# A hybrid attention and delta-rule layer: the fourth merged chunk transposed by DMA instead of by TensorE

## The reference, cut to what matters

```python
D_MODEL = 2048; SEQ = 256                      # x: (1, 256, 2048) float32
h = rms_norm(x, norm_gain)
aq, ak, av, az, bqkv, bz, bbeta, balpha, gate_a, gate_b = jnp.split(h @ w_in, cuts, axis=-1)
ya = moba_attention(heads(aq), heads(ak), heads(av)) * jax.nn.silu(az)          # 256 x 1024
yb = ...   # gated delta rule of bqkv, per-head RMSNorm, * silu(bz)              # 256 x 1024
merged = (jax.nn.sigmoid(gate_a) * (ya @ w_branch_a)
          + jax.nn.sigmoid(gate_b) * (yb @ w_branch_b))                          # 256 x 2048
x = x + merged @ w_out                                                           # 256 x 2048
return rms_norm(x, final_norm_gain)
```

## Time and profile before

| | |
|---|---|
| median of three runs | 771.9 us |
| the profiled execution | 772.16 us |
| its span in the profile | 770.4 us |
| TensorE busy | 758.4 us, 98% |
| VectorE / ScalarE / GpSimd busy | 73% / 60% / 16% |
| DMA queue of SyncE and ScalarE | 153.53 MB, 74% of the 16 engines' time |
| mean granted TensorE clock | 0.997 |

### The profile page before, as it was taken

One profiled execution on the slowest core, in us unless ns is written; L12 is line 12 of the kernel. 1 busy time (PEld: TensorE's weight loads), 2 busy tenths in 40 slices (PEclk: granted clock), 3 DMA queues, 4 the chain that ended last, 5 costly groups with the idle time before them and its releaser, 6 DMA issues.

```text
span 770.4 us, 10402 instructions
## 1 busy us (share of the span) xinstructions
PE 758.4 (98%) x3483; PEld 625.7 (81%) x3483; DVE 564.8 (73%) x1265; ACT 464.9 (60%) x697; POOL 122.1 (16%) x179
## 2 busy tenths in 40 slices
PE   8999999999999999999999999999999999999995
PEld 6888888888888888888888888888888888887884
DVE  5769847975895689479758956894798476966563
ACT  5686647656765675476657657764856663535441
POOL 6112011110101021101111120201021002512120
PEclk9999999999999999999999999999999999999998
DMA  9968767886788786778866786778676586798643
GB/s 254 241 170 219 205 163 214 193 217 179 184 209 198 192 208 181 199 192 197 212 174 203 200 217 170 203 188 215 174 213 182 181 222 182 217 331 268 190 153 109
DMA packets 225572, 154.44 MB, mean 200 GB/s; under 512 B 55408, under 2 KB 190576, under 8 KB 225392
## 3 DMA queue, kind: packets, MB, share of 16 engines
q1 hardware_dynamic: 225376, 153.53, 74.0%
q10 hardware_dynamic: 144, 0.26, 0.1%
HBM read 140.64 MB, written 2.11 MB: 185 GB/s over the span
## 4 chain that ended last, share of the span: by engine, by line
PE 95%; DMA 2%; issue 1%; DVE 1%; SPq 1%; ACT 0%; POOLq 0%; POOL 0%; DVEq 0%; ACTq 0%
PE pj L633 29%; PE pj L631 29%; PE pj L632 29%; DMA w_raw<-in_w_out_dram 1%; PE dn_ps L676 1%; PE pj L871 1%; PE pj L870 1%; PE pj L869 1%; DMA w_raw<-in_w_in_dram 1%; PE dn_ps L690 0%; PE dn_ps L685 0%; PE mo_ps L717 0%; PE dn_ps L677 0%; DVE w_lo L1169 0%; PE mo_ps L721 0%
## 5 line engine op out<-in xcount | busy, mean ns | idle before, releaser
L1169 DVE TENSOR_TENSOR w_lo<-w_raw,w_hi 128x1024 fp32r<-128x1024 f32 x251 | 312.6, 1250 | 138.1 <-ACT w_hi L885 137.1
L631 PE MATMUL pj<-w_hi,xt_hi 128*128 128x512 f32 x860 | 345.9, 402 | 1.2 <-DVE w_lo L1169 1.2
L633 PE MATMUL pj<-w_hi,xt_lo 128*128 128x512 f32 x860 | 336.6, 391 | 0.0
L632 PE MATMUL pj<-w_lo,xt_hi 128*128 128x512 f32 x860 | 335.8, 390 | 0.0
L885 ACT ACTIVATE w_hi<-w_raw 128x1024 fp32r<-128x1024 f32 x251 | 263.2, 1055 | 114.4 <-PE pj L633 88.3
L633 PEld LDWEIGHTS pj<-w_hi,xt_lo 128*128 128x128 f32 x860 | 161.4, 188 | 34.3
L631 PEld LDWEIGHTS pj<-w_hi,xt_hi 128*128 128x128 f32 x860 | 161.7, 188 | 33.5 <-issue 0.9
L632 PEld LDWEIGHTS pj<-w_lo,xt_hi 128*128 128x128 f32 x860 | 161.8, 188 | 31.4
L1356 DVE SCALAR_TENSOR_TENSOR xs<-lrep,xs 128x31 f32<-128x31 f32 (+30 forms) x496 | 88.9, 252 | 0.0
L550 POOL TENSOR_TENSOR xo<-v,own 128x128 f32<-128x128 f32 x16 | 13.6, 847 | 139.4 <-DVE v L1365 99.1
L1296 DVE SCALAR_TENSOR_TENSOR conv<-kk,hs,conv 128x255 f32<-128x255 f32 (+2 forms) x72 | 29.7, 480 | 0.0
(11 more groups left out here) (292 smaller groups left out, 760.6 us busy)
## 6 DMA issues: line engine op xcount, KB each, us to landing
w_raw<-in_w_in_dram SPq DMA_DIRECT2D x384, 256.0 KB, 3.3
w_raw<-in_w_out_dram SPq DMA_DIRECT2D x64, 256.0 KB, 4.0
w_raw<-in_w_branch_a_dram SPq DMA_DIRECT2D x32, 256.0 KB, 3.8
w_raw<-in_w_branch_b_dram SPq DMA_DIRECT2D x32, 256.0 KB, 3.7
gate<-in_x_dram SPq DMA_DIRECT2D x8, 256.0 KB, 5.2
gate<-in_x_dram SPq DMA_DIRECT2D x4, 512.0 KB, 7.7
gate<-in_final_norm_gain_dram SPq DMA_DIRECT2D x1, 1024.0 KB, 10.3
out_dram<-gate SPq DMA_DIRECT2D x4, 256.0 KB, 3.5
```

The costliest lines, as they stand in the source:

```text
L631: pe.matmul(bank[:, t, :], hi[:, k, tok], w_hi[:, slot, cs], start=(k == 0), stop=False)
L632: pe.matmul(bank[:, t, :], hi[:, k, tok], w_lo[:, slot, cs], start=False, stop=False)
L633: mm = pe.matmul(bank[:, t, :], lo[:, k, tok], w_hi[:, slot, cs], start=False, stop=(k == kt_all - 1))
L1169: dve.tensor_tensor(w_lo[:, slot, :], w_raw[:, slot, :], w_hi[:, slot, :].bitcast(F32), ALU.subtract).then_inc(lo_ready, 1)
```

## The change

Chunk 3 goes the way of chunks 0 to 2. M_TURNED gets a fourth entry, 231, so that the SyncE queue waits for the last m_apart behind the load of unit 231 and issues the DMA transpose there, ahead of the reload of x, the final gain and unit 232. GpSimd's loop runs over all four chunks. turn_merged_last, its semaphore and its PSUM operands are gone, and the final gain waits for m_apart, which the queue has waited for already.

```diff
-M_TURNED = [FIRST_B + BU * (c + 1) + 7 for c in range(NC - 1)]
+M_TURNED = [FIRST_B + BU * (c + 1) + 7 for c in range(NC)]
...
                     for j in range(NC):
                         sp.dma_start(gate[:, j, :, :], x[:, j * CH:(j + 1) * CH].rearrange("(t p) n -> p t n", p=P)
                                      ).then_inc(x_again, 16)
 
-                    sp.wait_ge(mT_done, 2)
+                    sp.wait_ge(m_apart, T * NC)
                     sp.dma_start(gate[:, NC:NC + NC // 2, :, :].rearrange("p c t n -> p (c t n)"),
...
             pool.wait_ge(vb_ready, T * H)
-            for c in range(NC - 1):
+            for c in range(NC):
                 for t in range(T):
                     pool.wait_ge(merged, T * c + t + 1)
...
-            def turn_merged_last():
-                pe.wait_ge(merged, T * NC)
-                for half in range(2):
-                    for q in range(4):
-                        i, t = 2 * half + q // 2, q % 2
-                        mm = pe.transpose(mo_ps[:, (4 * half + q) * P:(4 * half + q + 1) * P],
-                                          gate[:, 2 * NC - 1, t, i * P:(i + 1) * P], ident[:, :])
-                    mm.then_inc(mT_done, 1)
...
-                    if c == 0 and j == 2:
-                        turn_merged_last()
...
             def merged_hi(c):
                 for half in range(2):
-                    if c < NC - 1:
-                        act.wait_ge(m_joined, 2 * c + half + 1)
-                    else:
-                        act.wait_ge(mT_done, half + 1)
-                    m = (mT if c < NC - 1 else mo_ps)[:, half * CH:(half + 1) * CH]
+                    act.wait_ge(m_joined, 2 * c + half + 1)
+                    m = mT[:, half * CH:(half + 1) * CH]
...
             def merged_lo(c):
-                m = mT if c < NC - 1 else mo_ps
                 for half in range(2):
                     dve.wait_ge(mT_hi_ready, 2 * c + half + 1)
                     ks = slice(4 * c + 2 * half, 4 * c + 2 * half + 2)
-                    dve.tensor_tensor(xt_lo[:, ks, :].rearrange("p k t -> p (k t)"), m[:, half * CH:(half + 1) * CH],
+                    dve.tensor_tensor(xt_lo[:, ks, :].rearrange("p k t -> p (k t)"), mT[:, half * CH:(half + 1) * CH],
```

More of the change, by code:

```diff
@@ L260, in build @@
         m_apart, m_joined = sem("m_apart"), sem("m_joined")
-        mT_done, mT_hi_ready, mT_lo_ready = sem("mT_done"), sem("mT_hi_ready"), sem("mT_lo_ready")
+        mT_hi_ready, mT_lo_ready = sem("mT_hi_ready"), sem("mT_lo_ready")
         x_again = sem("x_again")
```

## The result

The changed kernel takes 778.48 us (median of four, 777.56 to 779.35) against 771.97 us for the kernel before beside it. The ratio over all executions is 1.0082, with a 95% interval of 1.0064 to 1.0100. The direction was as forecast, the size was not: 6.5 us instead of 2.9, and outside the range of 773.1 to 778.0. The profiled execution took 779.22 us with a span of 777.5 and a mean granted clock of 0.992, where the kernel before had 0.997; two of the four executions were near 779.3 at 0.992, two near 777.6 at 0.996.

A forecast was written before the change was run, and what follows sets the result against it. TensorE, busy 98% of the span, was taken to bound the kernel. 772.16 − 0.79 (transposes) + 0.65 (short waits) + 3.1 (wait before unit 232) = 775.1, median 0.26 lower, 774.8; range 773.1 to 778.0.

The forecast's parts named there:

- What bounds, and where: TensorE bounds, busy 98% of the span; its wait before unit 232 hangs on the SyncE queue and DMA engines.
- The chain to the transpose: GpSimd's m_apart complete at 682.65, x issued at 684.68, transpose landed at 687.07, unit 232 issued 4.56 us later.
- the 0.42 us to be saved: SyncE queue: the final gain no longer waits for mT_done, saving 0.42 us.
- a load of 256 KB: By the Trainium skill, the transpose would land like this w_out load, 4.0 us after issue instead of 4.4.
- The short waits: TensorE waits 0.15 us before unit 230 and 0.5 us before unit 231, 0.65 us added.
- their 0.79 us: Removing eight transposes from TensorE's path starts units 227 to 231 0.79 us earlier.
- What decides, the landing of unit 232: Its load lands 10.1 us after the transpose, at 697.2; unit 232 starts at 699.6, 2.9 us later than before.
- upper bound of 4.6: Unit 232's landing: at most the whole shift of its issue arrives, +4.6 us.
- The rival of the full shift: DMAs of x and the transpose hinder each other; unit 232 lands the whole 4.6 us later: 776.5, chance 0.12.
- The clock: Rival: TensorE's clock falls to half in the 3.7 us gap before unit 232, costing 1.95 us: 776.8, chance 0.22.
- The range: 773.1, where the lower bound begins to count, to 778.0, clock and the forecast's upper part together.

The follow-up runs named there:

- the wait alone: Kernel before, but GpSimd also takes chunk 3 apart, unused, and the SyncE queue waits for it, issuing no transpose: 775.63 us, 1.0052; again 776.79 us, 1.0052.
- two DMAs of x: Changed kernel with two of the four DMAs of x moved behind the loads of units 234 and 235: 775.0 us, 1.0039.
- the two kernels that fill the gap: Identity transposes on TensorE between units 231 and 232: 40 in the changed kernel, 776.45 us, 1.0066; 30 in the wait alone, 774.52 us, 1.0031.
- the unused transpose: The wait alone, with the SyncE queue also issuing the DMA transpose of chunk 3, whose result nobody uses: 778.1 us, 1.0083.
- the other source: Changed kernel with the four DMAs of x reading rows 0 to 255 of w_out instead, in the same shape: 778.29 us, 1.0081.
- the gain first: Changed kernel with the gain issued in front of the four DMAs of x instead of behind them: 780.42 us, 1.0095.
- x first: Changed kernel with the DMAs of x issued first, then the wait for m_apart, the DMA transpose, the gain and unit 232: 777.47 us, 1.0075.

## Why the prediction was wrong, point by point

- *What bounds, and where:* right. The loss sits at unit 232 and runs over the wait for m_apart, the issue of the transpose and the queue, as forecast. Taking x out of that place takes all of it away (0.9998).
- *The chain to the transpose:* right. Less the 0.5 us by which this execution runs later, x is issued at 684.6 (684.68 forecast) and the transpose lands at 687.0 (687.07). Unit 232 is issued 5.05 us later instead of 4.56: the issues of x and the gain took 0.51 us longer, which used up the 0.42 us to be saved. One comparison was off: the transpose moves all of m_halves, 128 x 2048 16-bit words or 512 KB, and the prediction set it beside a load of 256 KB. The sum did not use it.
- *The short waits:* right in the sum, not in the place. Unit 231 ends near 696.3, which is 695.85 and the offset. But the waits stand before units 228 (0.19 us) and 230 (0.32 us), none before unit 231. The prediction let unit 228 start at 684.25, although by the earlier trace rows the first half of xt_lo of chunk 2 is ready only at 683.83 + 0.65 = 684.48: the transposes on TensorE had covered a wait, so part of their 0.79 us could not be won.
- *What decides, the landing of unit 232:* here a term was mis-sized. I counted 10.1 us from the landing of whatever stands in front of x, since in the profile of before that was the time from unit 231's landing. Measured were 699.14 − (683.14 + 4.4) = 11.6. The model behind it, first in, first out, so that an emptier queue gives its share back, is what failed: with the queue all but empty it asks for some 10 us from the issue of x to unit 232, and 13.1 were measured (the wait alone), against 14.6 with the last loads of unit 231 in front. Of the 4.9 us by which x is issued later, 4.4 reach the landing (both less the offset), close to the prediction's own upper bound of 4.6. The rival of the full shift, at 0.12, was nearer than the forecast.
- *The clock:* a step of judgement failed. It had 0.22, because the gap would be 3.7 us and "nearly as long" as the one at the end of the kernel. The gap was 5.05, and it falls at 3.7 too: in the profile of the wait alone TensorE stood still for 3.72 us and the clock was 0.52 over 701.0 to 704.4. In the kernel with two DMAs of x it fell behind a wait of 3.06 us; in the first profile of the wait alone, behind 1.48 us, it did not. The price came out near, 1.95 us forecast, 1.8 and 2.3 measured by the two kernels that fill the gap, though its ground did not hold: the low stretch lasts 6.9 us and not 3.9, and a part of it lies in the wait itself, where it costs nothing. The Trainium skill (TensorE: Matmul & The Clock Gate, HAM oscillation) warned of such gaps, and these runs agree with it inside the kernel.
- *The range:* it held the full shift (776.5) and the clock (776.8) apart and never added them, though a longer gap is what makes the clock fall: the second follows from the first. Together they are 771.9 + 4.6 + 1.95 = 778.45, and 778.48 was measured. That the two agree so closely is luck, since executions of the changed kernel lie between 777.56 and 781.77. The upper end of 778.0 should have been at least that.

## What to carry to other kernels

Before a wait goes into a queue that issues DMAs, list what is queued behind it up to the first load that TensorE needs, and price the wait by the whole shift of that issue: having less in flight gave back 0.5 us of 4.9 here. See also what the removed work had covered: the first wait that comes up in its place takes its share of the saving. When a forecast has a gap on TensorE of several microseconds, the fall of the clock belongs to the same case as the gap, not beside it; and bulk transfers that nobody needs soon (x, the gain) belong behind the loads that are needed next, where a transpose in the same queue then cost nothing that could be told here (0.9998).

## What the runs showed of the hardware that I had not expected

- A DMA transpose behind 2 MB of transfers kept the SyncE queue in its issue for 7.49 us (1.3 to 3.3 in the other profiles) and so held up all behind it.
- The granted clock can fall after TensorE has gone back to work: behind the wait of 3.72 us it resumed at 699.99, and the clock, at 1.00 until 700.5, was at 0.50 from 701.0.
- How long it then stays low takes two values in the profiles: 6.8 to 6.9 us in five (both of the changed kernel, the unused transpose, the other source, the gain first), all with a mean clock of 0.992, and 3.4 to 3.5 us in three (the wait alone, x first, two DMAs of x), all with 0.994. What decides between them was not found.
- While the DMAs of x ran, the engines moved 179 and 256 GB/s in the changed kernel, with the transpose beside them at first, and 254 with an empty queue in the wait alone. They ran at 421 and 423 in the stretches behind that. With w_out as the source it was 236 over the first 6 us.
- The same transpose with the same loads around it (chunk 2) landed 4.4 us after its issue in some profiles and 5.9 us in others.
